# Sample attention of a hybrid decoder step: one sample at a time with keys as weights, or pairs of samples with queries as weights

## The reference, cut to what matters

```python
ck, cv = _nsa_compress(kv_c_full, wpos, wc, qk_g[1])      # 64 blocks of 64 keys
o_c, imp = _nsa_cmp_attend(q, qpos, ck, cv)               # compressed branch
idx = _nsa_select(imp, qpos, n_blocks)                    # 8 blocks per row and group
...
s = jnp.einsum('btgrd,btgkld->btgrkl', q, kb) * dh ** -0.5   # selected branch
p = _masked_softmax(s.reshape(B, T, G, R, -1), mask.reshape(B, T, G, 1, -1))
...
s = jnp.einsum('btgrd,bsgd->btgrs', q, kv[:, :, 0]) * dh ** -0.5   # window of 512 keys
mask = (kpos[None, :] >= 0) & (d >= 0) & (d < NSA_WINDOW)
...
o = gt[..., 0:1] * o_c + gt[..., 1:2] * o_s + gt[..., 2:3] * o_w
```

## Time and profile before

| | us |
|---|---|
| median of 3 runs | 4247.26 (4228.52 to 4252.52) |
| the profiled execution, its time | 4233.27 |
| its span | 4231.4 |
| PE busy | 3769.7 (89% of the span) |
| DVE, ACT, POOL busy | 1431.0, 546.9, 181.7 |

### The profile page before, as it was taken

How to read it: one execution, slowest core, us unless ns; L and a number is a source line. 1 busy time by engine, 2 the same in 40 slices (tenths; PEclk the granted TensorE clock), 3 DMA queues, 4 the chain that set the end, 5 groups by cost and what they waited for, 6 DMA issues and landing times. The chain is left out here.

```text
span 4231.4 us, 44095 instructions
## 1 busy us (share of the span) xinstructions
PE 3769.7 (89%) x17890; PEld 2507.1 (59%) x17890; DVE 1431.0 (34%) x3327; ACT 546.9 (13%) x1219; POOL 181.7 (4%) x279
## 2 busy tenths in 40 slices
PE   7998989999999999869888457676879999999998
PEld 4665666665677776658776443333446556665676
DVE  3445322233132232265564346542242213211111
ACT  1000011000111001111121024441011000100000
POOL 3111100000000000000000000000000000000000
PEclk8999999999999999866666658888999999999999
DMA  6565542322343323351221320004003333233443
GB/s 162 172 189 162 171 120 81 86 61 85 115 118 88 98 82 108 105 111 48 72 92 65 73 85 8 6 3 157 15 10 116 89 96 112 74 90 95 138 122 96
DMA packets 601110, 399.64 MB, mean 94 GB/s; under 512 B 90140, under 2 KB 577933, under 8 KB 596429
## 3 DMA queue, kind: packets, MB, share of 16 engines
q1 hardware_dynamic: 573084, 312.00, 27.1%
q0 software_dynamic: 13824, 67.12, 4.6%
q10 hardware_dynamic: 14000, 17.71, 1.2%
HBM read 364.80 MB, written 36.13 MB: 95 GB/s over the span
## 5 line engine op out<-in xcount | busy, mean ns | idle before, releaser
L400 PE MATMUL psum<-arena 128*128 128x384 f32 (+1 forms) x4224 | 1338.0, 475 | 24.3 <-DVE arena L535 15.8
L400 PEld LDWEIGHTS psum<-arena 128*128 128x128 f32 x4224 | 799.8, 192 | 493.2 <-issue 32.3
L410 PE MATMUL psum<-arena 128*128 128x384 f32 (+1 forms) x2112 | 662.1, 472 | 0.0
L410 PEld LDWEIGHTS psum<-arena 128*128 128x128 f32 x2112 | 399.9, 191 | 235.4 <-issue 4.8
L433 PE MATMUL psum<-arena 128*128 128x384 f32 (+3 forms) x816 | 271.4, 489 | 0.0
L549 DVE SCALAR_TENSOR_TENSOR arena<-arena,psum 128x384 f32<-128x384 f32 (+1 forms) x132 | 70.3, 532 | 582.0 <-ACT arena L487 581.8
L487 ACT ACTIVATE arena<-psum 128x384 f32<-128x384 f32 (+1 forms) x132 | 62.5, 473 | 1356.6 <-PE psum L400 1356.6
L565 DVE SCALAR_TENSOR_TENSOR arena<-psum,arena 128x384 f32<-128x384 f32 (+1 forms) x96 | 51.4, 536 | 506.6 <-PE psum L410 506.6
L558 DVE TENSOR_TENSOR arena<-psum,arena 128x384 f32<-128x384 f32 (+1 forms) x132 | 70.7, 536 | 423.0 <-PE psum L400 422.1
L433 PEld LDWEIGHTS psum<-arena 128*128 128x128 f32 (+1 forms) x816 | 153.2, 192 | 96.3 <-issue 19.5
L3406 PE MATMUL psum<-arena 128*128 128x128 f32 x528 | 87.6, 318 | 86.5 <-DVE arena L3503 54.1
(11 more groups left out here) (582 smaller groups left out, 3655.0 us busy)
## 6 DMA issues: line engine op xcount, KB each, us to landing
arena<-in_ffa_up SPq DMA_DIRECT2D x132, 512.0 KB, 5.2
arena<-in_ffb_up SPq DMA_DIRECT2D x132, 512.0 KB, 5.2
arena<-in_ffa_down SPq DMA_DIRECT2D x48, 704.0 KB, 4.5
arena<-in_ffb_down SPq DMA_DIRECT2D x48, 704.0 KB, 4.5
arena<-in_w_in SPq DMA_DIRECT2D x27, 1024.0 KB, 5.8
arena<-in_w_in SPq DMA_DIRECT2D x9, 1056.0 KB, 6.0
pT<-arena ACTq DMA_DIRECT2D x32, 192.0 KB, 5.3
arena<-xs SPq DMA_DIRECT2D x2, 2176.0 KB, 14.9
```

What stands on the lines that cost most here:

```text
L400: ins = mm(b[:, 0:n], w[:, g, k], hC[:, k, 0:n], start=(k == 0), stop=(k == KD - 1))
L410: ins = mm(b[:, 0:n], w[:, k], actT[:, k, 0:n], start=(k == 0), stop=(k == FH - 1))
```

## The change

Samples are taken in pairs u = 0 to 3 (samples 2u and 2u+1, x = 0, 1). A unit is now (u, c): c = 0 to 3 are 1024 past keys of both samples, c = 4 is the window of both. There are 20 units, one every two rounds, 56 rounds in all. Keys are turned as before. The scores are a product with the 64 queries of a sample as weights and 512 turned keys moving; sample x writes partitions 64x to 64x+63 of one bank, so the scores stand with query rows down the partitions. DVE adds the mask, scales and takes the running extreme in one instruction (`masked`), ACT takes the exponential of up to 1088 columns with its row sum in one instruction, PE turns the exponentials back in [128, 128] tiles (`turn_weights`), ACT copies them out, and they are the weights of the value products. Each unit keeps its own extreme; step 6 and 7 merge the units of a pair.

```diff
-        cache_in = [sem("cache_in0")]
+        cache_in = [sem(f"cache_in{i}") for i in range(2)]
...
-        SA_UNITS = sorted([(SA_FIRST + 6 * q + 3 * h, 0, q, h) for q in range(NB) for h in range(2)] +
-                          [(SA_FIRST + 6 * q + 1, 1, q, 0) for q in range(NB)])
-        SA_ROUNDS = SA_FIRST + 6 * NB - 3 + 8
+        SA_UNITS = [(u, c) for u in range(4) for c in range(5)]
+        SA_ROUNDS = SA_FIRST + 2 * len(SA_UNITS) + 6
...
+            units = [(v, r - SA_FIRST - 2 * v) for v in range(len(SA_UNITS))]
+            return [(v, s) for v, s in units if 0 <= s <= (7 if SA_UNITS[v][1] == 4 else 5)]
...
+        def sa_slot(v, x):
+            return (2 * v + x) % 6
```

PE, the new steps (the old `keys`, `scores`, `turned`, `spread_out`, `values`, `sums` go):

```diff
+            def scores(v, half):
+                u, c = SA_UNITS[v]
+                pe.wait_ge(rt.read, turned[v])
+                b = bank(rs)
+                for x in range(2):
+                    ins = mm(b[64 * x:64 * x + 64], QB[:, 2 * u + x], sKT[2 * x + half], start=True, stop=True, skip_group_check=True)
+                ins.then_inc(rs.full, 1)
...
+            def turn_weights(v):
+                u, c = SA_UNITS[v]
+                pe.wait_ge(scalar_for_tensor, pe.due(scalar_for_tensor))
+                n = 4 if c == 4 else 8
+                for half in range(n // 4):
+                    b = bank(rt)
+                    for t in range(4):
+                        j = (4 * half + t) * P
+                        ins = turn(b[:, t * P:(t + 1) * P], saS[:, j:j + P], ident)
+                    ins.then_inc(rt.full, 1)
...
+            def values(v, x):
+                u, c = SA_UNITS[v]
+                pe.wait_ge(rt.read, turned[v])
+                o = bank(rv)[64 * x:64 * x + 64, 0:P]
+                n = 4 if c == 4 else 8
+                for t in range(n):
+                    ins = mm(o, saPT[:, t, 64 * x:64 * x + 64], sVB[sa_slot(v, x)][:, t, P:2 * P],
+                             start=(t == 0), stop=(t == n - 1 and c < 3), skip_group_check=True)
...
+                if 2 in stage:
+                    scores(stage[2], 0)
+                if 4 in stage:
+                    values(stage[4], 0)
+                if 5 in stage:
+                    values(stage[5], 1)
+                if 2 in stage:
+                    if SA_UNITS[stage[2]][1] < 4:
+                        scores(stage[2], 1)
+                    if SA_UNITS[stage[2]][1] >= 3:
+                        new_scores(stage[2])
+                if 3 in stage:
+                    turn_weights(stage[3])
+                if 0 in stage:
+                    keys(stage[0], 0)
+                if 1 in stage:
+                    keys(stage[1], 1)
```

DVE and ACT:

```diff
-                op(e.tensor_reduce(x, st.rearrange("p t c -> p c t"), AX.X, ALU.max))
...
-                        op(e.tensor_tensor(st, st, sD[:, br].unsqueeze(1).broadcast_to([P, 4 if br else 16, 64]), ALU.subtract))
...
-                        op(e.tensor_reduce(sSM[:, br], st.rearrange("p t c -> p c t"), AX.X, ALU.add))
...
+            def masked(b, v, at, n, mask, first, ring):
+                u, c = SA_UNITS[v]
+                w = saW[:, u % 2, c, 0:1]
+                read(e.tensor_tensor_reduce(out=saS[:, at:at + n], in0=b[:, 0:n], in1=mask, scale=negs[:, 0:1],
+                                            scalar=(3e38 if first else w), op0=ALU.add, op1=ALU.min, accum_out=w), ring)
...
+                    done(a.activation(saS[:, 0:n], saS[:, 0:n], ACT.Exp, bias=w[:, 0:1], scale=-1.0, accum_out=w[:, 1:2]))
...
+            def weights(v):
+                c = SA_UNITS[v][1]
+                for half in range(1 if c == 4 else 2):
+                    b = full()
+                    read(a.copy(saPT[:, 4 * half:4 * half + 4], b.rearrange("p (t c) -> p t c", t=4)))
```

```diff
-            for h in range(8):
-                sp.eng.dma_start(GS[8 * h:8 * h + 8], pR[TP:R, PR_G + 3 * h:PR_G + 3 * h + 3].rearrange("(b t) c -> t b c", b=NB),
-                                 allow_slow_non_contiguous=True).then_inc(loads_for_vector, 16)
-                sp.eng.dma_start(sGB[8 * h:8 * h + 8], I["nsa_gate_b"][:, 3 * h:3 * h + 3].broadcast_to([8, 3]),
-                                 allow_slow_non_contiguous=True).then_inc(loads_for_vector, 16)
...
+                for v, s in sa_active(r):
+                    w = v + 3
+                    if s in (4, 5) and w < len(SA_UNITS) and SA_UNITS[w][1] < 4:
+                        gp.wait_ge(vector_for_gpsimd, gp.due(vector_for_gpsimd))
+                        gather(w, s - 4)
```

514 lines of the change are left out of this document (231 added, 283 removed).

## The result

| us | median | runs |
|---|---|---|
| kernel before | 4238.22 | 4 (4228.52 to 4252.52) |
| changed kernel | 4071.74 | 4 (4056.47 to 4076.86) |

The ratio is 0.9599, with a 95% interval of 0.9556 to 0.9642: faster by 4.0%, 166 us. The forecast was 4145, and its range ended at 4085. The profiled execution took 4074.01 us, its span is 4072.3, against 4231.4 before.

A forecast was written before the change was run, and what follows sets the result against it. PE was taken as the bound in the samples' attention (511 us, clock 0.67). Work 38, waits 22 and clock 38 made 98 us off 4233, 4135, plus 10 for the median: 4145 us; range for 8 in 10, 4085 to 4215.

The forecast's parts named there:

- the two smaller terms: Samples' attention stage: PE's work 38 us less at unchanged clock, and PE's idle time net 22 us less.
- the term of the clock: Samples' attention stage: PE's mean clock rises from 0.67 to 0.74, taking 38 us off.
- PE's work: Samples' attention: 132.2 us removed, 35.8 of turns and 58 of score products added; 38 us less at unchanged clock.
- 272 us at full clock: PE's remaining work in the samples' attention: 406 us at clock 0.67, restated at full clock.
- The pair of score products: Two 512-column products filling one bank's halves: 1.6 us per pair, 36 banks, 58 us; ends 46 and 133.
- rival 4: Score products' two halves do not overlap: 133 us in place of 58, about 4230 us; chance 0.04.
- Waits: PE in the samples' attention: 33.8 us of waits go, 12 put back for score bank, exponential and turn banks; net 22.
- Preparation and transfers: Gate loads and selection before the stage, and page gathers: both counted as 0; preparation's ends -5 and +5 us.
- Rounds: Attention takes 56 rounds instead of 63, no extra counted; DVE's busy share was separately put near 40%.
- rival 1: Samples' attention: clock follows the mixture and reaches the prompt attention's 0.84, 142 us less, 4091 us; chance 0.18.
- The argument against rival 1: Samples' attention: the lanes' products, mostly of 8 or 64 columns, fill a third of PE's time.
- rival 3: Samples' attention: 152 more turns and short waits hold the clock at 0.50, 78 us slower, 4311 us; chance 0.06.

The follow-up runs named there:

- b_double_scores: Kernel before with each 64-column score product issued twice, same result: 4302.36 us, ratio 1.0168.
- a_old_scores: Changed kernel with all 288 old narrow score products added back as dead work: 4142.78 us, ratio 0.9767 to the kernel before.
- a_old_gap: Changed kernel with 288 old score products as dead work and two extra 1.9 us DVE reductions per past-key unit: 4234.24 us, ratio 0.9999 to kernel before.
- b_both: Kernel before with the maximum reduced over 2 key tiles and each turn of a key tile issued twice: 4181.73 us, ratio 0.9859.
- a_gap: Changed kernel with two extra 1.9 us DVE reductions before the first masking of each of 16 past-key units: 4161.35 us, ratio 0.9812 to kernel before.
- b_double_turns: Kernel before with each turn of a key tile issued twice, 288 more turns: 4220.97 us, ratio 0.9964.
- a_old_gap_few: a_old_gap with one turn of exponentials per bank in place of four (36 for 144): 4258.43 us, ratio 1.0048 to the kernel before.
- b_wide_scores: Kernel before with one 256-column score product in place of four 64-column ones (72 for 288): 4193.76 us, ratio 0.9892.
- a_pair_values: Changed kernel with both samples' value products interleaved into two halves of one bank, next pages requested at step 4: 4058.61 us, ratio 0.9573 to kernel before.
- a_pair_order: a_pair_values with the turn of exponentials moved behind the turned keys of the round on PE and ACT: 4039.57 us, ratio 0.9519 to kernel before.

## Why the prediction was wrong

The direction and the two smaller terms held; the failing step is the term of the clock, "I take 0.74, between". It counted 38 us and measured 89 (99 if the clock is weighted by busy time), because the stage's clock was 0.86. By its steps:

- **PE's work.** "272 us at full clock" measured 269 (273 weighted). The pair of score products was taken at 1.6 us and is 1.27, but 1.6 was meant at the lower clock: 1.27 x 0.86 and 1.6 x 0.67 are 1.09 and 1.07 us at full clock. The two prompt rows were the right neighbours. The turned exponentials cost 0.145 us each where 0.235 was taken; at full clock these are 0.12 and 0.16. That the halves overlap (rival 4 denied) is shown.
- **Waits.** 22 us net foreseen, 28 measured. The score bank took 2.1 us in 3 waits. The place of the new wait was named wrongly in part: it is for the two turn banks, but in one wait of 7.0 us and 14 small ones, not evenly.
- **Preparation and transfers.** Counted at nothing, both right: the stage begins at 1884 as before, DVE's two waits only traded 5 us, and no wait of PE is for a page.
- **Rounds.** DVE's busy share was to be near 40% and is 44%.
- **The clock.** Two rows were read rightly, the falls after waits, and the estimate of what follows was too timid: falls after a wait went from 11 to 3, the full clock held for 78 and 59 us on end, and all falls together from 18 to 8. With the waits gone the prompt attention's 0.84 was named as an upper case (rival 1, 4091 us); the stage reached 0.86, and 4085 as the end of the range followed from taking 0.84 as a ceiling. That stage has its own waits, 101 of 350 us idle, and nothing made its level a ceiling. (Nor does the busy share alone set the level: b_double_scores is busy 90% of its stage at 0.71.) The argument against rival 1, that the lanes' small products fill a third of PE's time, did not hold: they are all still there at 0.86, and a_old_scores shows 0.87 with 576 more narrow records. It was not empty, though: the falls that are left begin mostly behind such products. The second cause was not seen at all: the added turns were counted as work and, in rival 3, as a danger, while in a stage that does have waits they shorten each fall.

With the level of 0.86 put into the prediction's own sum, 272/0.86 = 316 for PE, which is 128 less than 444, and its 22 less idle: 4233 - 150 = 4083, 9 us from the profiled 4074. The other terms were right to that much, and the clock alone accounts for most of the miss.

**Rival 3 and the rule behind it.** 152 more turns were to hold the clock down. The old kernel with 288 more turns went from 0.67 to 0.80, and taking 108 turns out of a_old_gap lowered it from 0.80 to 0.73. The Trainium skill, "TensorE: Matmul & The Clock Gate", section on the PE-mode transpose, says that the full clock does not engage in transpose mode; for single-precision turns among other products these runs do not bear it out: in the fall shown above the full clock returned while PE did nothing but turns. It is the measurement that decides.

What stays open. The levels of b_both and the changed kernel agree, but not their make-up: 16 falls of 8 us against 8 falls of 12 us. So b_both shows that shorter waits and more turns can lift the old kernel to 0.86, not that the change did it in that way. What the change did can be read off directly, fewer falls after a wait and shorter falls on the whole; that the missing waits are the cause of the first is supported by a_gap (from 3 such falls back to 18), and that the added turns are the cause of the second is argued, from b_double_turns and a_old_gap_few. a_old_gap_few has waits, old products and few turns, and stands at 0.73, not 0.67; the remaining 0.06 has no cause shown. Nor is it shown why taking the narrow score products out of the old kernel (b_wide_scores) brought falls down from 19 to 11 us, when putting them into the changed one did not lengthen them (12 and 12 us), and whether the lanes' products start the falls that have no wait ahead of them.

The clock of each stage is from one profiled execution, and among those of the changed kernel that hardly differ it lay between 0.86 and 0.90, so steps of 0.03 in the table should not be read as effects. For the larger steps the other executions can be asked, by the granted clock of their whole span: 0.89 to 0.90 in all of the kernel before, 0.91 in all five of b_double_turns, 0.91 to 0.92 in a_gap, 0.92 to 0.93 in the changed kernel.

## What to carry to other kernels

Split a stage into work at full clock, idle time and clock (busy time x PEclk, length less busy, the rest): the first two could be predicted from rows within a few us, and the third was the largest. Where a stage of PE has a granted clock well under 1, look in windows of 1 us at what stands ahead of each fall; in the changed kernel a regular wait of 3.5 us cost its own length and 2 to 3 us more for the half-speed stretch behind it, and one of 1.7 us did not. That is no safe size for other kernels: in the kernel before, a fall stood behind a wait of 1.46 us, with about 1 us more of idle time just ahead of it. Products that fill one half of the partitions should be issued alternately for the two halves; here that paid with 128 columns as with 512. But read the clock again after each such step: a_pair_values lost part of its gain to it.

## What the runs showed of the hardware that was not expected

- A wait of about 3 us in a stage at full clock was followed by 6 us at 0.50 with PE fully busy (a_old_gap, the windows above). Of the 89 us that the 16 waits of a_gap added to the changed kernel, 52 are waiting (idle time 39 to 91), and the other 37 or so are the clock.
- More work can be faster: 288 more turns took 17 us off the old kernel (ratio 0.9964, interval 0.9943 to 0.9985). The gain is small, but it stands where 35 us or more of added work would have been.
- Alternating the halves nearly halves value products of only 128 columns: 76.6 to 41.8 us for 576 records, with their count unchanged. Their weight loads fell with them, from 69.9 us busy in the changed kernel to 40.2 in a_pair_order, while the mean of one load rose from 147 to 159 ns. So the loads of the two halves overlap as well:

```profile
L2695 PEld LDWEIGHTS psum<-arena 128*64 128x64 f32 x576 | 69.9, 147 | 17.1 <-issue 16.1
```

```profile
L2697 PEld LDWEIGHTS psum<-arena 128*64 128x64 f32 x576 | 40.2, 159 | 15.8 <-issue 14.5 <-ACT arena L2794 0.9 <-ACT arena L2791 0.3
```
